# Three of the eight input tiles loaded from ScalarE's queue instead of the sync queue

## The reference

```
u = rmsnorm(h, attn_norm_g);  proj = u @ w_in            # 1024 x (512+128+128+512+512+512)
oa = sliding-window attention with sinks and T5 bias     # 8 query heads, 2 key heads
ob = differential attention with T5 bias                 # 4 heads, block-causal
h = h + concat(oa, ob) @ w_out
h = h + square(relu(rmsnorm(h) @ w_up)) @ w_down         # 4096 hidden
h = h + sigmoid(rmsnorm(h) @ w_gate) * (p @ w_ple)
y = rmsnorm(h, final_norm_g)
```

## Time and profile before

| what | value |
|---|---|
| median of 3 runs | 1265.87 us (1265.68 to 1266.86) |
| span of the profiled execution | 1264.6 us |
| median less that span | 1.27 us |
| TensorE busy | 1242.5 us, 98% |
| VectorE, ScalarE, GpSimd busy | 57%, 34%, 38% |
| first matmul of L1168 starts | 20.99 us |
| mean granted TensorE clock | 0.993 of full speed |

### The profile page before, as it was taken

How to read it: one execution, slowest core, us unless ns; L and a number is a source line. 1 busy time by engine, 2 the same in 40 slices (tenths; PEclk the granted TensorE clock), 3 DMA queues, 4 the chain that set the end, 5 groups by cost and what they waited for, 6 DMA issues and landing times.

```text
span 1264.6 us, 14755 instructions
## 1 busy us (share of the span) xinstructions
PE 1242.5 (98%) x5921; PEld 992.8 (79%) x5921; DVE 717.0 (57%) x974; ACT 426.6 (34%) x788; POOL 486.1 (38%) x231
## 2 busy tenths in 40 slices
PE   6999999999999999999999999999999999999997
PEld 5777777777677788888888888888888888888886
DVE  5255556566767355856847468376584672453234
ACT  7344435445565442212222122131221221342111
POOL 3221202222426682533524335244253352375643
PEclk8999999999999999999999999999999999999998
DMA  6811101112612231120220311202112012131203
GB/s 223 277 34 34 34 18 34 34 51 51 195 39 67 84 101 66 33 73 30 67 67 1 100 34 50 67 17 91 44 34 83 17 39 62 34 102 53 63 1 133
DMA packets 115258, 83.28 MB, mean 66 GB/s; under 512 B 21673, under 2 KB 103638, under 8 KB 115062
## 3 DMA queue, kind: packets, MB, share of 16 engines
q1 hardware_dynamic: 114806, 81.19, 20.9%
q10 hardware_dynamic: 384, 1.15, 0.2%
HBM read 73.91 MB, written 10.77 MB: 67 GB/s over the span
## 4 chain that ended last, share of the span: by engine, by line
PE 94%; DVE 2%; ACT 1%; issue 1%; DMA 1%; SPq 1%; DVEq 0%; ACTq 0%
PE ps L1146 35%; PE ps L1490 25%; PE ps L1168 23%; PE ps L1278 3%; PE ps L1301 3%; PE ps L1289 1%; PE ps L1365 1%; PE ps L1351 1%; PE ps L1338 1%; ACT e_a L895 1%; PE ps L1211 1%; DMA x_raw<-in_x 1%; PE ps L1182 0%; PE ps L1471 0%; DVE kmax L1777 0%
## 5 line engine op out<-in xcount | busy, mean ns | idle before, releaser
L720 POOL TENSOR_TENSOR w_lo<-w_raw,w_hi 128x1024 fp32r<-128x1024 f32 x63 | 152.7, 2423 | 310.1 <-ACT w_hi L801 310.1
L604 POOL TENSOR_TENSOR w_lo<-w_raw,w_hi 128x1024 fp32r<-128x1024 f32 x40 | 100.0, 2500 | 270.4 <-ACT w_hi L818 270.2
L1146 PE MATMUL ps<-z_hi,w_hi 128*128 128x512 f32 x624 | 193.3, 391 | 0.0
L1146 PE MATMUL ps<-z_hi,w_lo 128*128 128x512 f32 x624 | 192.2, 389 | 0.0
L1146 PE MATMUL ps<-z_lo,w_hi 128*128 128x512 f32 x624 | 192.2, 389 | 0.0
L1168 PE MATMUL ps<-u_hi,w_hi 128*128 128x512 f32 x416 | 177.2, 426 | 2.3 <-DVE o_bt L1719 1.7
L1490 PE MATMUL ps<-x_hi_op,w_hi 128*128 128x512 f32 x456 | 178.4, 391 | 0.0
L1490 PE MATMUL ps<-x_hi_op,w_lo 128*128 128x512 f32 x456 | 177.5, 389 | 0.0
L1490 PE MATMUL ps<-x_lo_op,w_hi 128*128 128x512 f32 x456 | 177.4, 389 | 0.0
L2042 DVE TENSOR_TENSOR h<-ps,h 128x512 f32<-128x512 f32 x224 | 144.8, 683 | 46.2 <-PE ps L1490 44.2
L1168 PE MATMUL ps<-u_hi,w_lo 128*128 128x512 f32 x416 | 164.1, 395 | 0.0
(11 more groups left out here) (182 smaller groups left out, 1680.7 us busy)
## 6 DMA issues: line engine op xcount, KB each, us to landing
w_raw<-in_w_up SPq DMA_DIRECT2D x64, 256.0 KB
w_raw<-in_w_in SPq DMA_DIRECT2D x48, 256.0 KB
w_raw<-in_w_down SPq DMA_DIRECT2D x18, 512.0 KB
raw_a<-in_w_down SPq DMA_DIRECT2D x14, 512.0 KB
x_raw<-in_x SPq DMA_DIRECT2D x8, 512.0 KB, 6.9
h_save<-x_t SPq DMA_DIRECT2D x1, 4096.0 KB, 12.3
h<-h_save SPq DMA_DIRECT2D x4, 1024.0 KB, 10.0
w_raw<-in_w_out SPq DMA_DIRECT2D x16, 256.0 KB
```

The source lines that it names most:

```text
L604: nc.gpsimd.tensor_tensor(w_lo[:, s * D:(s + 1) * D], w_raw[:, s * D:(s + 1) * D], w_hi[:, s * D:(s + 1) * D].bitcast(F32), ALU.subtract). ...
L720: nc.gpsimd.tensor_tensor(w_lo[:, s * D:(s + 1) * D], raw, w_hi[:, s * D:(s + 1) * D].bitcast(F32), ALU.subtract).then_inc(lo_done, 1)
L1146: mm = nc.tensor.matmul(o[i], w, xx[:, x0[i]], start=(first and n == 0), stop=(last and n == 2))
```

## The change

The sync queue keeps x0, x2, x4, x6 and x7 in their order, with all weights and small loads where they were. ScalarE issues x1, x3 and x5 as its first three instructions, ahead of `relb` and `hot`. Buffers, semaphores and every wait stay the same.

```diff
             for t in range(TT):
-                sp.dma_start(x_raw[:, t * D:(t + 1) * D], x[0, t * P:(t + 1) * P, :]).then_inc(x_in[t], 16)
+                if t % 2 == 0 or t >= 6:
+                    sp.dma_start(x_raw[:, t * D:(t + 1) * D], x[0, t * P:(t + 1) * P, :]).then_inc(x_in[t], 16)
                 if t == 0:
...
+            for t in (1, 3, 5):
+                act.dma_start(x_raw[:, t * D:(t + 1) * D], x[0, t * P:(t + 1) * P, :]).then_inc(x_in[t], 16)
             act.dma_start(relb[:, :], rel_bias).then_inc(hot_in, 16)
             act.dma_start(hot[:, :], onehot.rearrange("b c l -> b (c l)")).then_inc(hot_in, 16)
             square_x(0)
```

## The result

The changed kernel takes 1268.55 us (median of 12 runs, 1267.98 to 1269.19), the kernel before, run beside it, 1266.16 us (12 runs, 1265.53 to 1267.56). The ratio is 1.0018, 95% interval 1.0011 to 1.0026: 2.3 us slower, within the 0.2% that the prediction speaks of, and more than the scatter of these runs explains. The profiled execution has a span of 1266.5 us (before: 1264.6) and took 1268.3 us in all, so 1.8 us lie around it. One execution of a later kernel (e5) took 2079.34 us at a mean granted clock of 0.557; it is left out of that kernel's median and ratio, and no other execution here is of this kind.

A forecast was written before the change was run, and what follows sets the result against it. The head was taken to be bound by a computing chain starting when g_rows and x0 are there. Terms 0 + 0 + 1.05 + 0.3 = 1.35 us gave a span of 1265.95, plus 1.27 a time of 1267.2 us, range 1265.0 to 1269.0.

The forecast's parts named there:

- What bounds the head: Start of the kernel: a computing chain from g_rows and x0 sets the first big matmul at 20.99, not later x loads.
- The issues saved: Sync queue: three issues leave it, all behind x0 and g_rows, so later tiles come earlier; gain 0.
- rival 4: Head: the loads were the bound after all, start at most 0.6 us earlier, 1265.3 us; chance 0.06.
- Three issues at ScalarE's start: ScalarE: about 1.3 us of issues delay its small loads and table load, hidden by waiting and idling; cost 0.
- x0's share of the path: DMA path: x1 beside x0 costs 1.29 us, hot no longer beside it returns 0.24; net +1.05 us.
- The gain rows: Small g_rows loads behind x0: they take turns with x3's packets, +0.3 us, bounds 0 and +1.2.
- The sum: Head: x0's transposes 1.35 us later, passed on link by link, so the first big matmul starts at 22.3.
- the two cases I had named: Low clock after the start: rising still at 26.02 leaves 0.7 us of delay; rising equally long after leaves all 1.35.
- The step from span to time: Whole kernel: the median of the runs stands 1.27 us above the profiled span, 1265.95 giving 1267.2 us.
- Nothing moves: Head: x0's landing is start-up and the gain rows are set by their issue, 1265.9 us; chance 0.18.
- x0 behind all three tiles: DMA path: ScalarE's tiles go ahead of x0 or gain rows, transposes 3.9 us late, 1269.8 us; chance 0.10.
- The clock high at the start: First big matmuls run at 2.4 GHz, -2.5 us: 1264.7 us, or 1263.4 without a shift; chance 0.06.

The follow-up runs named there:

- e5: Kernel before with x3 and x5 issued from ScalarE behind the square of x0, x1 left in the sync queue: 1266.99 us, ratio 1.0003.
- e9: Kernel before with x0 transposed ahead of the gain rows and nothing else: 1265.54 us, ratio 0.9996.
- e2: Changed kernel with only x1 issued from ScalarE at its start, x3 and x5 back in the sync queue: 1268.01 us, ratio 1.0013.
- e4: Kernel before with the five gain loads issued from ScalarE ahead of its small loads, all of x on the sync queue: 1267.9 us, ratio 1.0013.
- e11: Changed kernel with one gain load behind x0 instead of five, the other four behind x7, gain rows transposed first: 1266.27 us, ratio 1.0003.
- e12: Changed kernel with three gain loads behind x0 instead of five, gain rows transposed first: 1268.06 us, ratio 1.0017.
- e6: Kernel before with x0 alone issued from ScalarE's queue and the five gain loads first in the sync queue: 1266.48 us, ratio 1.0001.
- e8: Changed kernel with one gain load instead of five ahead, the other four behind x7, and x0 transposed first: 1265.85 us, ratio 0.9999.
- e10: e6 with x0 also transposed before the gain rows: 1265.59 us, ratio 0.9995.
- e7: Kernel before with one gain load instead of five ahead, the other four behind x7, and x0 transposed first: 1265.95 us, ratio 0.9994.
- e3: Changed kernel with x0 transposed before the gain rows: 1266.66 us, ratio 1.0003.
- e1: Changed kernel with x1, x3 and x5 issued from ScalarE only behind the square of x0: 1268.12 us, ratio 1.0016.

## Why the prediction came out as it did

*What bounds the head.* Right. The chain from the gain rows and x0 through computing to the first big matmul carried the whole delay: 2.23 us at the transpose of the gain rows, 2.21 at the start. The issues saved and the tiles that came earlier were worth nothing, and rival 4 has no support. e9 adds that the other branch, TensorE's own transposes and bias products at the low clock, lies close behind: with the product 0.7 us sooner, the low part ends at 20.18 and TensorE's own work sets the start.

*Three issues at ScalarE's start.* Right: 1.37 us for the three, the table load at 3.29 to 4.57, the square of x0 when x0 is there, and ScalarE idle until 11.41. Cost 0.

*x0's share of the path.* Forecast +1.05, measured 5.43 - 4.53 = +0.90. Even turns, 91 packets against 88, are what the term supposed. The Trainium skill says as much in "DMA: Bandwidth & Descriptors", section "Queues, rings and completion order": each DMA engine goes round between the queue rows that it has work for, packet by packet; the trace agrees as long as both queues carry tiles. With the gain loads in the sync queue it counts 77 packets there against 252 from 5 to 7.5 us.

*The gain rows.* This is the mis-sized term: "I take +0.3, near the low end: their packets are few". Measured: (7.93 - 5.43) - (5.70 - 4.53) = 2.50 - 1.17 = +1.33, just beyond my upper bound of 1.2. 0.29 us of it is a later issue of the last load (2.87 instead of 2.58), as the load ahead of it took 0.59 us to issue; the rest passes after issue. Few packets were the wrong measure: the 33 packets needed 0.5 us before and 2.4 us now. The delay goes with having tiles on the other queue from the start (five loads are transposed at 5.70 to 5.80 without, at 7.6 to 8.0 with), be it three tiles or one (e2), and also with the small loads on ScalarE's queue and the tiles on the sync queue (e4). Fewer loads, issued sooner, shrink it (e11, e12). e6 is the exception.

*The sum.* Forecast 1.35 us at the start, measured 2.21. The square of x0 came as said (5.48), and each later mark (gains, product, low part of tile 3, start) 0.9 us later than said. The clock gave back 0.3 of it, between the two cases I had named. The step from span to time was off too: I took 1.27 us, the median less one profiled span; in every execution whose span is on record 1.7 to 1.9 us lie around it. With the measured terms, 1264.6 + 2.2 - 0.3 + 1.8 = 1268.3, the profiled execution's time. The median, 1268.55, is inside the range (1265.0 to 1269.0) since the range was wide, not since the term was right: 1267.2 was 1.35 us short.

*The rivals.* Nothing moves: no, the start moved by 2.21 us. x0 behind all three tiles: no, x0 came 0.90 us late, not 3.9. The clock high at the start: no, it was 0.50 (it was 1.00 in e8 and e10). That the gain rows are the later by far was in no rival; the forecast's shift of 0.7 to 2.4 us took it in only with the gain term at its upper bound, 1.05 + 1.2 = 2.25.

*Left open.* How the delay of a small load beside a stream is made up isn't settled. Two things are on record. In the changed kernel the packets themselves are spread out (4.82 to 7.22), and the semaphore is full 0.6 us after the last one starts. In e2 they pass at once (5.10 to 5.69), and the semaphore is full only 1.8 us later, where before it took 1.3. For the second, the Trainium skill, "DMA: Bandwidth & Descriptors", section "Queues, rings and completion order", states that a semaphore's increment lands only after every earlier write of that DMA engine, across its queues. It would fit e2; no run here shows which writes the increments waited for.

*A version that beats both.* e7, e9 and e10 stand below 1 by 0.0004 to 0.0006, but each interval includes 1, so none is shown to beat the kernel before. Against the changed kernel e3 and e6 to e11 do better by 1.9 to 3.0 us of medians, each taken beside other runs of before. Of these e3, e8 and e11 keep its three tiles on ScalarE's queue.

## What to carry to other kernels

Before moving a big load to a second queue, look for small loads that something early waits for. Here five of them, 16.5 KB in all, came 2.2 us later with tiles on the other queue from the start; with one load in place of five it was 0.3 us. Judge them by what is waited for and when it is issued, not by bytes. A load in the chain of waits is no proof that it bounds: follow what else the released instruction needs to its last arrival. And order work so that the wait for a late small load is covered (transposing x0 first brought the start 1.5 us forward here).

## What the runs showed of the hardware

- Two queues with tiles share the path packet by packet (91 and 88 packets in 2 us), and x0 lands 0.9 us later than without a tile on the other queue (5.43 against 4.53).
- A small load's packets can be through long before its semaphore is full: last packet at 5.69, semaphore full at 7.49 (e2).
- Five small loads (16.5 KB in all) on the otherwise empty ScalarE queue are used at 7.64 us beside the sync queue's stream, though the last was issued at 2.37 (e4).
- A tile issued at 4.63 into a path already full of weight loads took 6.9 us (e1), against 3.9 us for x0 in the same kernel, issued at the start.
- The same gain load took 0.59 us to issue instead of 0.29 with three tiles already issued by ScalarE, but 0.29 with one (e2). Why is not shown.
- With the clock at 0.50 for less time after the start, the span is shorter at the same start: 3.00 us of it against 5.03 gave 0.9 us (e9).
